# mLSTM head outputs: from "divide, square, normalise, gate" to "copy, square undivided, one factor with the gate"

## The chip, the cores and the metric

The kernel runs on one core of a Trainium2 chip. The metric is the device time of one execution in microseconds (us). TensorE (PE) multiplies matrices and writes its sums into PSUM, eight banks of 128 partitions by 512 fp32 numbers. VectorE (DVE), ScalarE (ACT) and GpSimd (POOL) work between PSUM and SBUF; SyncE's queue (SP) issues the transfers.

## The reference, cut to what matters

Two transformer blocks on 256 tokens of width 1024, all in fp32. The change lies in the first mixer of the second block, the mLSTM with four heads of 128 columns:

```
s   = einsum(q, k) * exp(d - m_t)
num = einsum(s, v) ;  den = sum(s)
h   = num / max(|den|, exp(-m_t))            # (256 tokens, 4 heads, 128)
hm  = rmsnorm(h, head_gain) * sigmoid(mo)    # mean of squares over the 128 columns of a head
out = concat([hm, stick_breaking_heads]) @ w_out
```

## The kernel before, in words

All tokens are handled at once, as two tiles (t = 0, 1) of 128 tokens on the 128 partitions. Every weight matrix comes through a ring of four 1 MB slots (SP, line 251) and is split into a high and a low part of reduced precision, in parts of 128x1024: ACT copies the high part (line 279), DVE subtracts to get the low part (line 282), and PE makes three products per tile of weights (line 303 for products that give columns, lines 365 and 383 for products that give rows). PE is in order and so are the others, and each engine's list is written out by hand.

The mixer's stage is a list of slots s = 0 to 18 (`ab_pe`, `ab_act`, `ab_dve`). In each slot ACT and DVE first split one weight part (the one that PE uses some parts later), and then do a step of the heads that is due there. PE runs one part of a weight product and then `after(s)`, the heads' small matmuls. Slots 0 to 7 go with eight parts of the product with the weights of the stick-breaking queries and keys, slots 8 to 11 with the row product `ab_sv`, slots 12 to 18 with the row product `ab_out`, which takes the heads' outputs as its left side. Heads n = 0 to 3 are mLSTM, 4 to 7 stick-breaking.

The names that matter:

- `first(n)`, `second(n)` (lines 1322 to 1342): a head's first two small products, into banks 4 and 5. `weigh(n)` (lines 1354 to 1356): the head's weights times its values, into bank 6: for an mLSTM head 2 x 129 columns, the 129th being `den`. Since there is one bank 6, `weigh(n)` waits until `ab_o` says that head n-1 has been taken out.
- `finish(n)` on DVE, in slots 3 to 6: takes bank 6 out. It makes `max(|den|, exp(-m_t))` in two small instructions (lines 1565, 1567), its reciprocal (1568), and one multiply for each tile out of the bank (1570); the last of them raises `ab_o`.
- `head_squares_dve` in slot 7: two squares of 128x512 (1610) and two sums (1611), each waited for, and then `ab_ssq`. ACT makes `exp(-0.5 ln(mean + eps))` of it (1480, 1481) and only then goes on to slot 8, whose first work is the split of the last part of `ab_sv`.
- `head_gate_dve` in slots 8 and 9, one tile in each: times the norm's factor (1618), times the gate `SGM` (1619), then `ab_om`.
- `turn(c)` on PE after slots 10 and 11 (1373): transposes heads c and c+1 of both tiles; it waits for `ab_om` = 2, for both c. `turn(0)` stands in PE's list ahead of the last 24 matmuls of `ab_sv` (line 383), and ahead of it stands `first(6)` (1326), which waits for the last weight part of `ab_sv` (line 282, slot 8). ACT (`high`, 1453) and DVE (`low`, 1576) take the turned heads out.

Of the kernel before, what the change touches and what calls it, by code (L numbers as in the profile page):

```python
# [5 lines left out]
P = 128  # L6
T = 256
TT = T // P
# [11 lines left out]
ALU = mybir.AluOpType  # L20
ACT = mybir.ActivationFunctionType
# [81 lines left out]
def build_two_blocks(nc, I, out):  # L103
# [9 lines left out]
    with ExitStack() as ctx:  # L113
# [93 lines left out]
        def named(name):  # L207
            if name not in S:
                S[name] = sem(name)
            return S[name]  # L210
# [3 lines left out]
        def act_then(ins):  # L214

            chain_n["act"] += 1
            ins.then_inc(s_act_chain, 1)
            nc.scalar.wait_ge(s_act_chain, chain_n["act"])
# [1052 lines left out]
        L3 = MIX[:, 768:1536].rearrange("p (a n) -> p a n", a=2)  # L1271
        SP3 = view(70 * 256, (2, 384))
        W3 = view(73 * 256, (2, 384))
        HSQ = view(65 * 256, (TT, 4, P))
        HST = view(69 * 256, (4, 8))
        GC = view(62 * 256, (TT, 36))
        DN = view(63 * 256, (4, 2, 2))
        SQK_TILE = (0, 4, 2, 6)
        NSL = 12
        FIRST_AT = {0: 0, 1: 1, 2: 2, 3: 3, 5: 4, 6: 5, 9: 6, 11: 7}  # L1280
# [14 lines left out]
        def ab_pe():  # L1295
# [67 lines left out]
                mm.then_inc(named("ab_pv"), 1)  # L1363

            def turn(c):
                pe.wait_ge(named("ab_om"), 2)
                if c:
                    pe.wait_ge(named("ab_tl"), 1)
                else:
                    pe.wait_ge(named("ab_row"), 5)  # L1370
                for i in range(2):
                    for t in range(TT):
                        mm = pe.transpose(PS[:, 7, i * T + t * P:i * T + (t + 1) * P],
                                          OM2[:, t, (c + i) * P:(c + i + 1) * P], ident[:, :])
                mm.then_inc(named("ab_tp"), 1)
# [40 lines left out]
        def ab_act():  # L1416
            cols_done(act, "ab_mqk", 0)
            act.activation(ABT[:, 8:10, :], PS[:, A, :].rearrange("p (c n) -> p c n", c=2),
                           ACT.Copy).then_inc(named("ab_ca"), 1)
            split_through(act, "ab_g", 3)  # L1420
            act.wait_ge(named("ab_row"), 1)
            act.activation(ROWSG[0:4, 1, :], ROWSG[0:4, 0, :], ACT.Tanh, scale=1.0 / 15).then_inc(named("ab_log"), 1)
            act.preload_act_table_set(EXP_LN)
            act.wait_ge(named("ab_row"), 2)
            act_then(act.activation(ROWSG[0:4, 4, :], ROWSG[0:4, 3, :], ACT.Exp))
            act.activation(ROWSG[0:4, 5, :], ROWSG[0:4, 4, :], ACT.Ln, bias=one_c[0:4, 0:1]).then_inc(named("ab_log"), 1)
            split_through(act, "ab_g", 4)
            act.wait_ge(named("ab_row"), 3)
            act.activation(GA[32:36, :], ROWSG[0:4, 9, :], ACT.Exp, scale=-1.0).then_inc(named("ab_log"), 1)
            for t in range(TT):  # L1430
                rows_done(act, "ab_vo", 2 * t + 1)
                act.activation(SGM[:, t, :], PS[:, G + 2 * t + 1, :], ACT.Sigmoid).then_inc(named("ab_sgm"), 1)
            act.preload_act_table_set(EXP_LN)

            def soft(n):
                act.wait_ge(named("ab_u"), n + 1)
                if n < 4:
                    act.activation(L3[:, n % 2, :], U3[:, n % 2, :], ACT.Exp).then_inc(named("ab_l"), 1)
                    return
                if n >= 6:  # L1440
                    act.wait_ge(named("ab_sp"), n - 5)
                act_then(act.activation(L3[:, n % 2, :], U3[:, n % 2, :], ACT.Abs))
                act_then(act.activation(L3[:, n % 2, :], L3[:, n % 2, :], ACT.Exp, scale=-1.0))
                act.activation(L3[:, n % 2, :], L3[:, n % 2, :], ACT.Ln, bias=one_c[:, 0:1]).then_inc(named("ab_l"), 1)

            def exp_w(n):
                act.wait_ge(named("ab_sec_read"), n + 1)
                act.wait_ge(named("ab_pv"), n - 1)
                act.activation(W3[:, n % 2, :], U3[:, n % 2, :], ACT.Exp).then_inc(named("ab_w"), 1)

            def high(c):
                act.wait_ge(named("ab_tp"), c // 2 + 1)
                act.activation(ab_group(0, c), PS[:, 7, :].rearrange("p (c n) -> p c n", c=2),
                               ACT.Copy).then_inc(named("ab_th"), 1)

            def out_high(n):
                act.wait_ge(named("ab_pv"), n + 1)
                act.activation(ab_t(0, n), PS[:, 6, 0:T], ACT.Copy).then_inc(named("ab_oh"), 1)

            base = first_part[first_unit["ab_sqk"]]  # L1460
            for s in range(NSL + DC - 1):
                split(act, base + s + 3)
                if s < 8 and s % 2:
                    u, tile = s // 2, SQK_TILE[s // 2]
                    act.wait_ge(s_used, base + s + 1)
                    act.activation(ABT[:, tile:tile + 2, :], PS[:, u, :].rearrange("p (c n) -> p c n", c=2), ACT.Copy,
                                   scale=(1.0 if tile >= 4 else P ** -0.5)).then_inc(named("ab_ca"), 1)
                if s == NSL - 1:
                    for t in range(TT):
                        rows_done(act, "ab_sv", t)  # L1470
                        act.activation(SV[:, t, :], PS[:, G + t, :], ACT.Copy).then_inc(named("ab_svr"), 1)
                if s in EXP_W_AT:
                    exp_w(EXP_W_AT[s])
                if s in AB_WEIGH_AT and AB_WEIGH_AT[s] >= 4:
                    out_high(AB_WEIGH_AT[s])
                if s in FIRST_AT:
                    soft(FIRST_AT[s])
                if s == AB_SSQ_AT:
                    act.wait_ge(named("ab_ssq"), 1)
                    act_then(act.activation(HST[:, 1, :], HST[:, 0, :], ACT.Ln, bias=eps_c[:, 0:1], scale=1.0 / P))  # L1480
                    act.activation(HST[:, 2, :], HST[:, 1, :], ACT.Exp, scale=-0.5).then_inc(named("ab_hrs"), 1)
                if s in AB_TURN_AT:
                    high(AB_TURN_AT[s])

        def ab_dve():
# [73 lines left out]

            def finish(n):  # L1560
                dve.wait_ge(named("ab_pv"), n + 1)
                o = PS[:, 6, 0:258].rearrange("p (t n) -> p t n", t=2)
                dn = DN[:, n, :, :]

                dve_then(dve.scalar_tensor_tensor(out=dn[:, 0, :], in0=o[:, :, 128], scalar=-1.0,
                                                  in1=GC[:, :, 32 + n], op0=ALU.mult, op1=ALU.max))
                dve_then(dve.tensor_tensor(dn[:, 0, :], o[:, :, 128], dn[:, 0, :], ALU.max))
                dve_then(dve.reciprocal(dn[:, 1, :], dn[:, 0, :]))
                for t in range(TT):
                    ins = dve.tensor_scalar(OM2[:, t, n * P:(n + 1) * P], o[:, t, 0:P], dn[:, 1, t:t + 1], None,  # L1570
                                            ALU.mult)
                ins.then_inc(named("ab_o"), 1)

            def low(c):
                dve.wait_ge(named("ab_th"), c // 2 + 1)
# [9 lines left out]
            for s in range(NSL + DC - 1):  # L1585
# [7 lines left out]
                if s in AB_FINISH_AT:  # L1593
                    finish(AB_FINISH_AT[s])
                if s == AB_SSQ_AT:
                    dve.wait_ge(named("ab_o"), 4)
                    head_squares_dve(OM2, HSQ, HST, 4, "ab_ssq")
                if s in AB_GATE_AT:
                    dve.wait_ge(named("ab_hrs"), 1)
                    dve.wait_ge(named("gate_gain"), 2)  # L1600
                    head_gate_dve(OM2, AB_GATE_AT[s], HST, 4, SGM, "ab_om")
                if s in AB_TURN_AT:
                    low(AB_TURN_AT[s])
                if s in AB_WEIGH_AT and AB_WEIGH_AT[s] >= 4:
                    out_low(AB_WEIGH_AT[s])

        def head_squares_dve(o_all, sq, st, heads, told):
            for t in range(TT):
                o = o_all[:, t, :].rearrange("p (h d) -> p h d", h=heads)
                dve_then(dve.tensor_tensor(sq[:, t, :, :], o, o, ALU.mult))  # L1610
                dve_then(dve.tensor_reduce(st[:, 0, heads * t:heads * (t + 1)], sq[:, t, :, :], AX.X, ALU.add))
            dve.sem_inc(named(told), 1)

        def head_gate_dve(o_all, t, st, heads, gate, done):

            o = o_all[:, t, :].rearrange("p (h d) -> p h d", h=heads)
            r = st[:, 2, heads * t:heads * (t + 1)].unsqueeze(2).to_broadcast([P, heads, P])
            dve_then(dve.tensor_tensor(o, o, r, ALU.mult))
            dve.tensor_tensor(o, o, gate[:, t, :].rearrange("p (h d) -> p h d", h=heads),
                              ALU.mult).then_inc(named(done), 1)  # L1620

        def gate_gain_pool(gate, gain, heads, sem_name, per_tile, told):

# [1179 lines left out]
```

## Time and profile before

| | |
|---|---|
| median of 3 runs | 1328.74 us (1327.57 to 1329.91) |
| profiled execution, its own time | 1329.45 us |
| its span, first to last instruction | 1327.6 us |
| mean granted clock of TensorE | 0.985 of full |
| the mixer's slots 0 to 18, in the span | about 447 to 532 us |

The profiled execution took 0.71 us more than the median of the runs, and 1.85 us of its time lie outside its span. Sums of instruction times are made against the profiled execution; the median is used to place them among the runs.

### The profile page before, as it was taken

What the parts mean: (1) busy time and instruction counts of PE and PEld (TensorE: products, weight loads), DVE (VectorE), ACT (ScalarE), POOL (GpSimd) and SP (SyncE); (2) the same over time, 40 slices, a digit from 0 to 9 for tenths busy, and PEclk for the clock granted to TensorE, in tenths of its full rate; (3) what the DMA queues carried; (4) which work ended last, traced back from release to release, by engine and by line L of the source; (5) the groups of instructions that cost most, each with busy time, mean ns of one, the idle gap of its engine ahead of it and who ended that gap; (6) DMA issues with size and microseconds to landing.
All of it is one profiled execution on the core that took longest, in us unless ns stands there. A gap on an engine that the chain in (4) does not pass through costs nothing.

```text
span 1327.6 us, 22040 instructions
## 1 busy us (share of the span) xinstructions
PE 1271.8 (96%) x9160; PEld 1152.9 (87%) x9160; DVE 792.4 (60%) x1163; ACT 707.6 (53%) x1118; POOL 128.3 (10%) x146
## 2 busy tenths in 40 slices
PE   6999999999999989999999999998999999999997
PEld 6988899998888877888999888987998888999886
DVE  5786678885456555645555446786645635655444
ACT  6767666664476534644655335554355634655433
POOL 6000001110000000000111000105600000111000
PEclk9999999999999998999999999998999999999999
DMA  9433465555544523543555555532203534465550
GB/s 335 161 117 107 143 191 187 176 180 196 188 138 175 190 69 137 175 143 112 169 182 189 191 177 159 183 120 92 92 8 111 190 128 139 149 189 190 191 191 32
DMA packets 141430, 205.52 MB, mean 155 GB/s; under 512 B 3730, under 2 KB 118802, under 8 KB 141330
## 3 DMA queue, kind: packets, MB, share of 16 engines
q1 hardware_dynamic: 141330, 204.11, 46.5%
q8 instruction: 72, 1.18, 0.4%
q14 instruction: 28, 0.23, 0.0%
HBM read 203.05 MB, written 1.05 MB: 154 GB/s over the span
## 4 chain that ended last, share of the span: by engine, by line
PE 84%; DVE 7%; ACT 5%; issue 2%; POOL 1%; DMA 1%; SPq 0%; DVEq 0%; ACTq 0%; POOLq 0%
PE ps L303 40%; PE ps L365 27%; PE ps L383 5%; PE ps L2080 2%; DVE weights_lo L282 2%; PE ps L1705 1%; ACT weights_hi L279 1%; PE ps L2142 1%; PE ps L1727 1%; PE ps L487 1%; POOL arena L2368 1%; DVE split_arena L518 1%; ACT normed L904 1%; DMA weights<-in_w_in 1%; PE ps L755 0%
## 5 line engine op out<-in xcount | busy, mean ns | idle before, releaser
L282 DVE TENSOR_TENSOR weights_lo<-weights,weights_hi 128x1024 fp32r<-128x1024 f32 x379 | 471.4, 1255 | 253.5 <-ACT weights_hi L279 251.3
L303 PE MATMUL ps<-split_arena,weights_hi 128*128 128x256 f32 x3056 | 561.8, 286 | 8.5 <-DVE split_arena L518 6.8
L279 ACT ACTIVATE weights_hi<-weights 128x1024 fp32r<-128x1024 f32 x379 | 396.7, 1056 | 274.3 <-PE ps L365 182.7
L303 PEld LDWEIGHTS ps<-split_arena,weights_hi 128*128 128x128 f32 x3056 | 479.3, 193 | 17.2 <-issue 12.0
L303 PE MATMUL ps<-split_arena,weights_lo 128*128 128x256 f32 x1528 | 433.4, 284 | 0.0
L303 PEld LDWEIGHTS ps<-split_arena,weights_lo 128*128 128x128 f32 x1528 | 294.4, 193 | 0.0
L365 PE MATMUL ps<-weights_hi,split_arena 128*128 128x512 f32 x992 | 272.7, 392 | 2.4 <-ACTq L1877 1.6
L365 PEld LDWEIGHTS ps<-weights_hi,split_arena 128*128 128x128 f32 x992 | 184.5, 188 | 41.7 <-issue 2.9
L365 PE MATMUL ps<-weights_lo,split_arena 128*128 128x512 f32 x496 | 153.7, 390 | 0.0
L365 PEld LDWEIGHTS ps<-weights_lo,split_arena 128*128 128x128 f32 x496 | 93.1, 188 | 19.7
L1885 POOL TENSOR_TENSOR normed<-normed 128x512 f32<-128x512 f32 x32 | 34.1, 1065 | 502.0 <-ACTq L1877 502.0
L1893 DVE TENSOR_TENSOR split_arena<-normed,split_arena 128x512 fp32r<-128x512 f32 x32 | 22.2, 693 | 73.8 <-POOL normed L1885 73.8
L383 PE MATMUL ps<-weights_hi,split_arena 128*128 128x512 f32 x192 | 62.6, 399 | 0.0
L1875 ACT ACTIVATE normed<-ps 128x512 f32<-128x512 f32 x32 | 19.1, 597 | 53.5 <-PE ps L303 53.5
L1188 POOL TENSOR_TENSOR arena<-arena 128x512 f32<-128x512 f32 x11 | 21.9, 1993 | 257.9 <-ACT arena L1133 163.1
L1171 DVE SCALAR_TENSOR_TENSOR arena<-ps,conv_cols,arena 128x255 f32<-128x255 f32 (+1 forms) x88 | 38.4, 478 | 13.7 <-ACT arena L1145 12.9
L383 PEld LDWEIGHTS ps<-weights_hi,split_arena 128*128 128x128 f32 x192 | 37.2, 194 | 7.9
L1145 ACT ACTIVATE arena<-ps,conv_cols 128x256 f32<-128x256 f32 x44 | 22.4, 560 | 37.8 <-PE ps L303 37.8
L303 PE MATMUL ps<-mem_t_hi,weights_hi 128*128 128x256 f32 x128 | 38.2, 299 | 3.3 <-DVE weights_lo L282 3.3
L518 DVE SCALAR_TENSOR_TENSOR split_arena<-ps,ln_cols,split_arena 128x256 fp32r<-128x256 f32 x72 | 29.5, 475 | 16.8 <-ACT split_arena L501 16.8
L2409 DVE SCALAR_TENSOR_TENSOR arena<-ps,cconv_cols,arena 128x255 f32<-128x255 f32 (+2 forms) x72 | 31.4, 477 | 13.4 <-ACT arena L2234 12.5
L383 PE MATMUL ps<-weights_lo,split_arena 128*128 128x512 f32 x96 | 38.3, 399 | 0.0
(364 smaller groups left out, 1321.3 us busy)
## 6 DMA issues: line engine op xcount, KB each, us to landing
weights<-in_mlp_w SPq DMA_DIRECT2D x64, 1024.0 KB, 5.3
weights<-in_w_up SPq DMA_DIRECT2D x22, 1024.0 KB, 5.1
weights<-in_c_w_in SPq DMA_DIRECT2D x16, 1024.0 KB, 5.4
weights<-in_w_in SPq DMA_DIRECT2D x14, 1024.0 KB, 6.3
weights<-in_ab_w_in SPq DMA_DIRECT2D x12, 1024.0 KB, 5.3
weights<-in_w_down SPq DMA_DIRECT2D x11, 1024.0 KB, 4.9
weights<-in_xa_wv SPq DMA_DIRECT2D x8, 1024.0 KB, 4.9
weights<-in_xa_wq SPq DMA_DIRECT2D x8, 1024.0 KB, 5.2
```

The source lines that it names most:

```text
L279: act.activation(h, r, ACT.Copy).then_inc(s_hi, 1)
L282: dve.tensor_tensor(l, r, h.bitcast(F32), ALU.subtract).then_inc(s_lo, 1)
L303: mm = pe.matmul(o, w[:, k, :], x[:, k, :], start=(k == 0 and i == 0), stop=(k == DC - 1 and i == 2))
L365: mm = pe.matmul(PS[:, banks[nb * t + b], :], x[:, t * P:(t + 1) * P], w[:, c:c + 512], start=(k == 0 and i == 0), stop=False)
L383: mm = pe.matmul(PS[:, banks[nb * t + b], :], x[:, t * P:(t + 1) * P], w[:, c:c + 512], start=(k == 0 and i == 0), stop=(k == chunks - 1 a ...
L518: ins = dve.scalar_tensor_tensor(out=dst[1][:, k, :], in0=PS[:, turn_bank(m) + c2, c * T:(c + 1) * T], scalar=ln_cols[:, gain, k:k + 1], i ...
L1145: ins = act.activation(CS[:, u % 4, f, :], PS[:, G + u % 4, f * T:(f + 1) * T], ACT.Identity, bias=c[:, 3:4], scale=c[:, 2:3])
L1171: ins = dve.scalar_tensor_tensor(out=CS[:, u % 4, f, lag:T], in0=PS[:, G + u % 4, f * T:(f + 1) * T - lag], scalar=c[:, tap:tap + 1], in1= ...
L1885: pool.tensor_tensor(RSQ[:, u % 2, :, :], RLU[:, u % 2, :, :], RLU[:, u % 2, :, :], ALU.mult).then_inc(named("m1_f"), 1)
L1893: dve.tensor_tensor(HID[1][:, 2 * u:2 * u + 2, :], RSQ[:, u % 2, :, :], HID[0][:, 2 * u:2 * u + 2, :].bitcast(F32), ALU.subtract).then_inc ...
L2080: mm = pe.matmul(PS[r, bank + hg, 64 * m:64 * m + 64], lhs(r, hg, m), rhs(r, hg, m), start=True, stop=True)
L2409: ins = dve.scalar_tensor_tensor(out=CC[:, u % 4, f, lag:T], in0=PS[:, G + u % 4, f * T:(f + 1) * T - lag], scalar=cconv_cols[:, TILE[u] + ...
```

## The change

`finish(n)` becomes one copy of the whole bank region, 258 columns, to the new tile `RAW`; the copy raises `ab_o`. Behind it DVE squares and sums the undivided numerators of the head, one `tensor_tensor_reduce` for each tile of tokens, which leaves the 128 squares in `OM2` (not used) and the sum in `HST`. `head_means` in slot 7 makes the four heads' denominators, reciprocals and mean squares together in five instructions on 128x8 numbers, since the norm of a divided head is that of the undivided one times the reciprocal squared. ACT's two small instructions stay. `head_gates(g)` in slots 8 and 9 multiplies norm factor and reciprocal into one factor for each head and tile, and applies it and the gate in one `scalar_tensor_tensor` per head and tile: heads 0 and 1 of both tiles in slot 8, heads 2 and 3 in slot 9 (before: all heads of tile 0, then of tile 1). `turn(0)` waits for the first of these groups only.

```diff
@@ -1271,10 +1271,10 @@
         L3 = MIX[:, 768:1536].rearrange("p (a n) -> p a n", a=2)
         SP3 = view(70 * 256, (2, 384))
         W3 = view(73 * 256, (2, 384))
-        HSQ = view(65 * 256, (TT, 4, P))
-        HST = view(69 * 256, (4, 8))
+        RAW = view(65 * 256, (4, TT, 129))
+        HST = view(69 * 256 + 16, (5, 4, TT))
         GC = view(62 * 256, (TT, 36))
-        DN = view(63 * 256, (4, 2, 2))
+        DN = view(63 * 256, (2, 4, TT))
         SQK_TILE = (0, 4, 2, 6)
         NSL = 12
         FIRST_AT = {0: 0, 1: 1, 2: 2, 3: 3, 5: 4, 6: 5, 9: 6, 11: 7}
@@ -1363,7 +1363,7 @@
                 mm.then_inc(named("ab_pv"), 1)
 
             def turn(c):
-                pe.wait_ge(named("ab_om"), 2)
+                pe.wait_ge(named("ab_om"), c // 2 + 1)
                 if c:
                     pe.wait_ge(named("ab_tl"), 1)
                 else:
@@ -1477,8 +1477,9 @@
                     soft(FIRST_AT[s])
                 if s == AB_SSQ_AT:
                     act.wait_ge(named("ab_ssq"), 1)
-                    act_then(act.activation(HST[:, 1, :], HST[:, 0, :], ACT.Ln, bias=eps_c[:, 0:1], scale=1.0 / P))
-                    act.activation(HST[:, 2, :], HST[:, 1, :], ACT.Exp, scale=-0.5).then_inc(named("ab_hrs"), 1)
+                    act_then(act.activation(HST[:, 3, :, :], HST[:, 2, :, :], ACT.Ln, bias=eps_c[:, 0:1],
+                                            scale=1.0 / P))
+                    act.activation(HST[:, 4, :, :], HST[:, 3, :, :], ACT.Exp, scale=-0.5).then_inc(named("ab_hrs"), 1)
                 if s in AB_TURN_AT:
                     high(AB_TURN_AT[s])
 
@@ -1559,17 +1560,39 @@
 
             def finish(n):
                 dve.wait_ge(named("ab_pv"), n + 1)
-                o = PS[:, 6, 0:258].rearrange("p (t n) -> p t n", t=2)
-                dn = DN[:, n, :, :]
-
-                dve_then(dve.scalar_tensor_tensor(out=dn[:, 0, :], in0=o[:, :, 128], scalar=-1.0,
-                                                  in1=GC[:, :, 32 + n], op0=ALU.mult, op1=ALU.max))
-                dve_then(dve.tensor_tensor(dn[:, 0, :], o[:, :, 128], dn[:, 0, :], ALU.max))
-                dve_then(dve.reciprocal(dn[:, 1, :], dn[:, 0, :]))
+                dve.tensor_copy(RAW[:, n, :, :],
+                                PS[:, 6, 0:258].rearrange("p (t n) -> p t n", t=TT)).then_inc(named("ab_o"), 1)
+                dve.wait_ge(named("ab_o"), n + 1)
                 for t in range(TT):
-                    ins = dve.tensor_scalar(OM2[:, t, n * P:(n + 1) * P], o[:, t, 0:P], dn[:, 1, t:t + 1], None,
-                                            ALU.mult)
-                ins.then_inc(named("ab_o"), 1)
+                    h = RAW[:, n, t, 0:P]
+                    ins = dve.tensor_tensor_reduce(out=OM2[:, t, n * P:(n + 1) * P], in0=h, in1=h, scale=1.0, scalar=0.0,
+                                                   op0=ALU.mult, op1=ALU.add, accum_out=HST[:, 0, n, t:t + 1])
+                if n == 3:
+                    dve_then(ins)
+
+            def head_means():
+                den = RAW[:, :, :, 128]
+                dve_then(dve.scalar_tensor_tensor(out=DN[:, 0, :, :], in0=den, scalar=-1.0,
+                                                  in1=GC[:, :, 32:36].rearrange("p t n -> p n t"),
+                                                  op0=ALU.mult, op1=ALU.max))
+                dve_then(dve.tensor_tensor(DN[:, 0, :, :], den, DN[:, 0, :, :], ALU.max))
+                dve_then(dve.reciprocal(DN[:, 1, :, :], DN[:, 0, :, :]))
+                dve_then(dve.tensor_tensor(HST[:, 1, :, :], HST[:, 0, :, :], DN[:, 1, :, :], ALU.mult))
+                dve.tensor_tensor(HST[:, 2, :, :], HST[:, 1, :, :], DN[:, 1, :, :],
+                                  ALU.mult).then_inc(named("ab_ssq"), 1)
+
+            def head_gates(g):
+                if g == 0:
+                    dve.wait_ge(named("ab_hrs"), 1)
+                    dve_then(dve.tensor_tensor(DN[:, 0, :, :], HST[:, 4, :, :], DN[:, 1, :, :], ALU.mult))
+                    dve.wait_ge(named("gate_gain"), 2)
+                for n in (2 * g, 2 * g + 1):
+                    for t in range(TT):
+                        cols = slice(n * P, (n + 1) * P)
+                        ins = dve.scalar_tensor_tensor(out=OM2[:, t, cols], in0=RAW[:, n, t, 0:P],
+                                                       scalar=DN[:, 0, n, t:t + 1], in1=SGM[:, t, cols],
+                                                       op0=ALU.mult, op1=ALU.mult)
+                ins.then_inc(named("ab_om"), 1)
 
             def low(c):
                 dve.wait_ge(named("ab_th"), c // 2 + 1)
@@ -1593,31 +1616,13 @@
                 if s in AB_FINISH_AT:
                     finish(AB_FINISH_AT[s])
                 if s == AB_SSQ_AT:
-                    dve.wait_ge(named("ab_o"), 4)
-                    head_squares_dve(OM2, HSQ, HST, 4, "ab_ssq")
+                    head_means()
                 if s in AB_GATE_AT:
-                    dve.wait_ge(named("ab_hrs"), 1)
-                    dve.wait_ge(named("gate_gain"), 2)
-                    head_gate_dve(OM2, AB_GATE_AT[s], HST, 4, SGM, "ab_om")
+                    head_gates(AB_GATE_AT[s])
                 if s in AB_TURN_AT:
                     low(AB_TURN_AT[s])
                 if s in AB_WEIGH_AT and AB_WEIGH_AT[s] >= 4:
                     out_low(AB_WEIGH_AT[s])
-
-        def head_squares_dve(o_all, sq, st, heads, told):
-            for t in range(TT):
-                o = o_all[:, t, :].rearrange("p (h d) -> p h d", h=heads)
-                dve_then(dve.tensor_tensor(sq[:, t, :, :], o, o, ALU.mult))
-                dve_then(dve.tensor_reduce(st[:, 0, heads * t:heads * (t + 1)], sq[:, t, :, :], AX.X, ALU.add))
-            dve.sem_inc(named(told), 1)
-
-        def head_gate_dve(o_all, t, st, heads, gate, done):
-
-            o = o_all[:, t, :].rearrange("p (h d) -> p h d", h=heads)
-            r = st[:, 2, heads * t:heads * (t + 1)].unsqueeze(2).to_broadcast([P, heads, P])
-            dve_then(dve.tensor_tensor(o, o, r, ALU.mult))
-            dve.tensor_tensor(o, o, gate[:, t, :].rearrange("p (h d) -> p h d", h=heads),
-                              ALU.mult).then_inc(named(done), 1)
 
         def gate_gain_pool(gate, gain, heads, sem_name, per_tile, told):
 
```

## Rows read from the trace of the kernel before

**Rows 1.** The page, part 4: the chain that ended last, by engine.

```profile
PE 84%; DVE 7%; ACT 5%; issue 2%; POOL 1%; DMA 1%; SPq 0%; DVEq 0%; ACTq 0%; POOLq 0%
```

**Rows 2.** Waits of PE, 440 to 532 us: us in total, times, longest.

```profile
PE ps L1373 <- DVE arena L1619: 4.1, 1, 4.1
PE ps L1354 <- DVE arena L1570: 3.0, 2, 1.8
PE ps L1326 <- DVE weights_lo L282: 1.0, 1, 1.0
PE ps L1336 <- DVEq L1544: 0.6, 1, 0.6
```

**Rows 3.** Windows of the stage: stretch, busy by engine, then PEclk, the granted clock.

```profile
450.00:458.50 8.50, 7.91 (x52) 6.85 (x51) 5.45 (x8) 4.22 (x7) 0.00 (x0) 1.00 0.37 123
...
468.00:472.50 4.50, 3.61 (x17) 3.64 (x18) 3.52 (x10) 1.14 (x2) 0.00 (x0) 0.62 0.25 36
...
501.00:509.50 8.50, 8.50 (x29) 6.93 (x30) 2.34 (x4) 2.82 (x5) 0.00 (x0) 0.67 0.34 123
```

**Rows 4.** Timeline of PE: start, us, line, what it is.

```profile
495.85 0.70 PE L1326 MATMUL ps<-arena 128*128 128x256 f32 x2 [1.04 <-DVE weights_lo L282]
```

**Rows 5.** The chain in order of time: start, us, what.

```profile
468.89 0.67 PE ps L1354 x2
...
470.42 3.79 PE ps L303 x24
...
480.26 0.46 PE ps L1354 x2
...
481.17 2.87 PE ps L303 x24
...
500.88 1.11 PE ps L1373 x4
501.99 7.63 PE ps L383 x24
...
511.15 0.44 PE ps L1373 x4
511.58 5.46 PE ps L365 x24
```

**Rows 6.** Timeline of DVE, same columns as group 4.

```profile
467.55 0.15 DVE L1565 SCALAR_TENSOR_TENSOR arena<-ps,arena 128x2 f32<-128x2 f32 x1
...
468.13 0.61 DVE L1570 TENSOR_SCALAR arena<-ps,arena 128x128 f32<-128x128 f32 x2
...
490.11 0.68 DVE L1610 TENSOR_TENSOR arena<-arena 128x512 f32<-128x512 f32 x1
...
495.72 0.55 DVE L1556 SCALAR_TENSOR_TENSOR normed<-ps,normed 128x384 f32<-128x384 f32 x1
...
500.13 0.69 DVE L1619 TENSOR_TENSOR arena<-arena 128x512 f32<-128x512 f32 x1
```

**Rows 7.** Timeline of ACT, same columns as group 4.

```profile
493.05 0.30 ACT L1480 ACTIVATE arena<-arena,eps_c 128x8 f32<-128x8 f32 x1 [2.30 <-DVEq L1612]
...
493.50 1.05 ACT L279 ACTIVATE weights_hi<-weights 128x1024 fp32r<-128x1024 f32 x1
...
499.53 0.52 ACT L1442 ACTIVATE normed<-normed 128x384 f32<-128x384 f32 x1 [1.76 <-DVE normed L1533]
...
502.11 0.58 ACT L1453 ACTIVATE split_arena<-ps 128x512 fp32r<-128x512 f32 x1
```

**Rows 8.** DVE by line and form over the span: count, busy, mean ns, idle before.

```profile
L1021 DVE CUSTOM_DVE_ANT_0 normed<-ps,arena 128x128 f32<-128x128 f32 x20 | 5.7, 285 | 0.0
...
L1021 DVE DVE_READ_ACCUMULATOR2_ANT arena<- 128x1 f32 x40 | 3.3, 83 | 0.0
...
L1651 DVE COPY arena<-ps 128x256 f32<-128x256 f32 x5 | 2.1, 419 | 4.5 <-PE ps L303 4.5
...
L1036 DVE SCALAR_TENSOR_TENSOR normed<-normed,arena 128x128 f32<-128x128 f32 x4 | 1.4, 348 | 0.1
```

## The prediction, made before the changed kernel was run

> **What bounds the kernel now.** I read the page's chain first: PE holds 84% of what ended last [rows 1], so what counts in a stage is where PE stands still, and at which clock it runs. Then PE's waits in the changed stage, 440 to 532 us. There are five stops, 8.8 us together [rows 2]: 4.1 us ahead of turn(0) (line 1373), for the second tile's gate; 3.0 us in two stops ahead of weigh(1) and weigh(3) (1354), for the divide of the head before; 1.0 us ahead of first(6) (1326), for a weight split; 0.6 us ahead of a second(n) (1336), which the change doesn't touch. Then the granted clock: 1.00 from 450 to 458.5 us, but 0.62 from 468 to 472.5 and 0.67 from 501 to 509.5 [rows 3], part of each stretch at the lower of the two levels (1.2 instead of 2.4 GHz). Both times PE had just stood: 1.19 us (what 3.0 leaves beside the 1.85 ahead of weigh(3); the times of the stops follow from the rows of DVE and the chain) and 4.10 us. The chain gives the price as the same work at both levels [rows 5]. Last I read DVE's and ACT's timelines, for what is late ahead of each stop [rows 6, 7].
>
> **The copy out of the bank.** Before, DVE's finish takes from 467.55 to 468.74 (468.13 plus 0.61) [rows 6], and weigh(1) starts at 468.89 [rows 5], 0.15 later. Now one copy stands there. The nearest row is a copy of 128x256 out of PSUM, 0.42 us [rows 8]; two more columns add nothing that matters. The bank is free at 467.55 + 0.42 = 467.97, and PE starts at 468.12: **0.77 us** gained. The third finish has the same form, so weigh(3) gains the same, **0.76 us**. The two stops shrink to about 0.4 and 1.1 us. If the copy cost as much as a 128x512 instruction (0.68 [rows 6]), 0.5 would be left of each gain; so 0.5 to 0.8 each.
>
> **The squares behind the copy.** Two instructions of the kind at line 1021, 0.285 us at 128x128, each with a read of the accumulator, 0.083 [rows 8]. End to end that is 0.74 us at most; overlapped as the neighbours in the timeline overlap (0.08 each), about 0.55. With the copy and a wait for it, some 1.05 to 1.25 us, against 1.19 before: DVE is as long in finish as it was, but bank 6 is no longer behind it. What would be late next is the DVE split of the next slot; it isn't later than before.
>
> **The means.** head_squares runs from 490.11 [rows 6], and ACT's Ln starts at 493.05 [rows 7]: 2.94 us with the handover, of which 0.08 is the handover. Now there are five small chained instructions on 128x8. Three of that kind took from 467.55 to 468.13 [rows 6], 0.193 each, so 0.97 together (0.8 if only the instructions counted, 1.25 if strided operands cost a quarter more). Ln starts at 490.11 + 0.97 + 0.08 = 491.16, which is 1.89 earlier. ACT's two small ones and the split that stands behind them [rows 7], and then DVE's split, all come 1.89 earlier. The split ended at 495.79 before (PE starts 0.06 later, 495.85 [rows 4]), so at 493.9 now. PE is through with its preceding matmuls at 495.85 - 1.04 = 494.81: it doesn't wait, and the whole stop ahead of first(6) goes, **1.04 us**.
>
> **The gates.** first(6) then runs from 494.81 to 495.74 (it took from 495.85 to 496.78, the 4.10 us ahead of 500.88 taken off). DVE: after_second(5), at 495.72 before [rows 6], is at 493.83 and ends at 494.30 (0.55 less the overlap); one small product, 0.2; four scalar_tensor_tensor of 128x128, 0.348 each by line 1036 [rows 8], 0.27 apart with the overlap: 1.16. The first group is done at 495.66, end to end without overlap at 496.0. PE was released at 500.88 by an instruction that ended at 500.82 [rows 5, 6]; now it is released at 495.72 to 496.1, against its own 495.74. So 4.10 us become 0 to 0.35; I take 0.2 and a gain of **3.9 us**. Three things make it: less work in slot 7, only half of the gating ahead of turn(0), and that slot 9's split and after_first(6), which stood between the two gate calls, are no longer ahead of it. DVE's work over the whole change is about 10 us before and 8.5 after; alone it would be worth nothing.
>
> A rule that speaks against eight short gates instead of four long ones: the Trainium skill, "VectorE: DVE Perf Modes", section "The TRN2 errata", says that each instruction on SBUF operands pays a fixed latency, so that large tiles are to be preferred. The trace agrees: 0.348 us for 128 columns against 0.69 for 512. By rule and row the gating takes 2.8 us as it did before; it is the order and not the amount that I count on.
>
> **The clock.** From 468.89 to 470.42 PE did weigh(1) at the lower level, 1.53 us; the same at the higher one is 480.26 to 481.17, 0.91. The 24 matmuls behind took 3.79 against 2.87 [rows 5]. Together 1.54 us. After turn(0)'s stop: 1.11 against 0.44 and 7.63 against 5.46, together 2.84 us [rows 5]. If nothing of the long stop is left, the second goes; I take **2.8 us**. For the first, the row to go by is the stop of 0.6 us ahead of line 1336 [rows 2], after the same kind of small matmuls on 4 and 64 rows: the clock stayed at 1.00 [rows 3]. The stop is 0.4 now, so I take that it stays up, **1.5 us**. The Trainium skill, "TensorE: Matmul & The Clock Gate", section "What's actually happening", has it that the lower level is the default and that activity releases it; by that the second is given back, and of the first it says less than the row.
>
> **What could be late next.** PE now comes to the end of line 383's matmuls 7 us sooner than DVE and ACT were used to. Between first group and low(0) they have: DVE's split of slot 9, after_first(6), the second gate group; ACT's soft(6), its split and high(0), which took from 499.53 to 502.69 [rows 7]; then DVE's split, after_l(6), low(0). Put one behind another from 495.7, with 1.2 us for a DVE split (the distance of 2.67 from Ln to after_second less ACT's 0.45 and 1.05) and 0.5 for the short ones: soft(6) starts at 497.7, high(0) ends at 500.9, low(0) ends at about 502.7. PE needs sp(6) at 495.9 + 0.4 + 5.5 + 0.6 = 502.4 and the low part at 503.3. That is just enough. In slot 12 the same chain is some 0.2 us late ahead of second(7). I count **0.3 us** lost, 0 to 3.
>
> **The sum.** 0.77 + 0.76 + 1.04 + 3.9 + 1.5 + 2.8 - 0.3 = 10.5 us. The profiled execution took 1329.45 us, so 1318.95, its span 1317.1. That execution was 0.71 above the median of 1328.74; from the median it is 1318.2. I forecast **1318.5 us**. The transfers don't bind here: each weight slot is asked for four units ahead, and no stop of PE in the stage ends with a DMA [rows 2].
>
> **The rivals.**
> - The clock falls once all the same, after what is left of weigh(1)'s stop or somewhere new, since a shift by 10 us moves all later work: 1.5 to 2.8 us less, **1320 to 1321.5**. For it: it fell after only 1.19 us. Against: the stop of 0.6.
> - DVE and ACT become the bound of slots 9 to 12, by the thin margin above; the stop moves to second(6), turn(2) or second(7). 3 us, and with them a stretch at the lower level, 1.5: **1321.5 to 1323.5**. A stop in the same place by a gate group that is a microsecond longer than by my rows gives the same.
> - It is slower: the new square instruction is much dearer between a copy and a wait than at line 1021. Place: behind the copy in slots 3 to 6, where eight of them stand ahead of the DVE splits that PE needs. The gains of 10.5 are used up, and more, when eight cost over 1.4 us each beyond their 0.29 (11.2 us in all, if nothing covers them): at 2 us each, **1332**. Nothing in the rows of line 1021 speaks for it.
> - No change: turn(0) is released no sooner, as something else than the gates holds it. Then only the copy and the first clock stretch count, 1 to 3 us, **1326 to 1328**. Against: PE's stop ends 0.06 us after the last gate.
>
> **How the numbers follow.** Forecast 0.60, 1316.5 to 1320. Clock once 0.20; late chain 0.13; no change 0.05, slower 0.02. The range, 1315.5 to 1323.0, takes in the first three but for their edges; below it is what a luckier clock in the rest of the kernel could give, one stretch of 1.5. A change of 0.2% (2.7 us) is about what measurements of this kernel can tell from none. Faster 0.95, same 0.03, slower 0.02.
>
> **What would show it.** PE's waits in the stage: the 4.1 ahead of turn(0) under 0.5, none ahead of first(6), about 0.4 and 1.1 ahead of weigh(1) and weigh(3). ACT's Ln about 1.9 us sooner after after_second(4). The granted clock 1.00 from weigh(1) to turn(2). If a new stop stands ahead of second(6), turn(2) or second(7), the second rival holds. The forecast is wrong if the first gate group ends over 0.5 us behind first(6), or if the clock falls without a stop.

## The result

The changed kernel takes 1319.70 us (median of 4 runs, 1317.09 to 1321.31), the kernel before 1329.33 us in the runs beside it (4 runs, 1327.57 to 1330.22): a ratio of 0.9927, 95% interval 0.9907 to 0.9948, so 9.6 us or 0.7% faster. The profiled execution of the changed kernel took 1320.48 us, with a span of 1318.8.

PE's waits in the same stage of the changed kernel (us in total, times, longest), to be read against [rows 2]:

```profile
PE ps L1354 <- DVE arena L1563: 1.5, 2, 1.1
PE ps L1336 <- DVEq L1545: 0.6, 1, 0.6
PE ps L1373 <- DVE arena L1592: 0.3, 1, 0.3
```

The stop ahead of turn(0) is 0.3 in place of 4.1 us, that ahead of first(6) is gone, the two ahead of weigh(1) and weigh(3) are half as long, and the one that the change didn't touch is as it was. Stops in the stage went from 8.8 to 2.4 us.

The windows of the changed kernel (busy by engine, then the granted clock), against [rows 3]:

```profile
450.00:521.40 71.40, 68.95 (x409) 59.80 (x408) 43.14 (x83) 34.64 (x53) 0.00 (x0) 1.00 0.39 128
468.00:472.50 4.50, 4.08 (x35) 3.96 (x34) 3.54 (x13) 1.52 (x3) 0.00 (x0) 1.00 0.16 15
```

The granted clock is 1.00 from end to end of the stage.

The whole times differ between runs of these two kernels by 3 and 4 us (by up to 7 for a variant below), so the stage is measured by itself, in the profile: from the start of the last 24 matmuls of `ab_vo`, the row product just ahead of slot 0 (line 383), to the start of the last 24 of `ab_out`. The stage of the two kernels was measured twice and repeats to 0.01 us, that of the variants below once. The chain of the kernel before (start, us, what) has the first here, the first matmuls of weigh(2), and the group that ends where the second begins, at 528.78 + 2.75 = 531.53:

```profile
441.68 5.45 PE ps L383 x24
...
474.21 0.23 PE ps L1354 x2
...
528.78 2.75 PE ps L365 x12
```

and the chain of the changed kernel:

```profile
442.14 5.45 PE ps L383 x24
...
468.57 0.46 PE ps L1354 x2
...
469.47 2.88 PE ps L303 x24
472.35 0.23 PE ps L1354 x2
...
477.63 0.46 PE ps L1354 x2
...
493.10 0.66 PE ps L1373 x4
493.76 5.48 PE ps L383 x24
...
500.76 0.44 PE ps L1373 x4
...
521.47 5.44 PE ps L383 x24
```

The stage takes 531.53 - 441.68 = 89.85 us before and 521.47 - 442.14 = 79.33 after: **10.52 us less**, against a forecast sum of 10.5.

### The profile page after: what moved, and what is told of

The parts are those of the page before. It is cut to its first block, busy times and chain, and to the rows that moved or that the text cites. A ratio compares the mean times of both kernels' runs of the same rounds, so it can differ in the third digit from the quotient of the medians.

```text
span 1318.8 us, 22045 instructions
## 1 busy us (share of the span) xinstructions
PE 1271.2 (96%) x9160; PEld 1152.8 (87%) x9160; DVE 789.5 (60%) x1169; ACT 707.4 (54%) x1118; POOL 127.7 (10%) x146
## 3 DMA queue, kind: packets, MB, share of 16 engines
HBM read 203.05 MB, written 1.05 MB: 155 GB/s over the span
## 4 chain that ended last, share of the span: by engine, by line
PE 84%; DVE 7%; ACT 5%; issue 2%; POOL 1%; DMA 1%; SPq 0%; DVEq 0%; ACTq 0%; POOLq 0%
PE ps L303 41%; PE ps L365 27%; PE ps L383 5%; DVE weights_lo L282 2%; PE ps L2085 2%; PE ps L1710 1%; ACT weights_hi L279 1%; PE ps L2147 1%; PE ps L1732 1%; PE ps L487 1%; POOL arena L2373 1%; DVE split_arena L518 1%; ACT normed L904 1%; DMA weights<-in_w_in 1%; PE ps L755 0%
## 5 line engine op out<-in xcount | busy, mean ns | idle before, releaser
L365 PE MATMUL ps<-weights_lo,split_arena 128*128 128x512 f32 x496 | 153.7, 390 | 0.0
L2373 POOL TENSOR_TENSOR arena<-arena,level_masks 64x512 f32<-64x512 f32 x24 | 34.1, 1420 | 42.2 <-DVEq L2483 34.6
```

Source lines behind the costliest of these rows:

```text
L365: mm = pe.matmul(PS[:, banks[nb * t + b], :], x[:, t * P:(t + 1) * P], w[:, c:c + 512], start=(k == 0 and i == 0), stop=False)
L2373: ins = pool.tensor_tensor(LT[r, lvl % 2, hg, :, :], ATC[r, hg, :, r], LM[r, lvl, r].unsqueeze(1).to_broadcast([64, 8, 64]), ALU.mult)
```

## Where the 10.5 us are, and the rest

The same chain gives the terms one by one, each as the distance between two starts, before and after:

| from, to | before | after | gained | forecast |
|---|---|---|---|---|
| start to weigh(1): its stop | 27.21 | 26.43 | 0.78 | 0.77 |
| weigh(1) to weigh(2): the clock | 5.32 | 3.78 | 1.54 | 1.5 |
| weigh(2) to weigh(3): its stop | 6.05 | 5.28 | 0.77 | 0.76 |
| weigh(3) to turn(0): two stops | 20.62 | 15.47 | 5.15 | 4.94 |
| turn(0) to turn(2): the clock | 10.27 | 7.66 | 2.61 | 2.8 |
| turn(2) to the end: late chain | 20.38 | 20.71 | -0.33 | -0.3 |

The last row is where the forecast had it, ahead of second(7) (line 1341) in slot 12. second(7) waits for a step of DVE (line 1551) that ends at 506.60; it starts 0.10 us late and takes 0.88 in place of 0.65:

```profile
506.75 0.88 PE ps L1341 x2
```

DVE and ACT, to see that the steps are those of the forecast (timelines of the changed kernel, start, us, line, what, idle before it):

```profile
468.00 0.42 DVE L1563 COPY arena<-ps 128x258 f32<-128x258 f32 x1
468.45 0.29 DVE L1568 CUSTOM_DVE_ANT_0 arena<-arena 128x128 f32<-128x128 f32 x1
468.67 0.08 DVE L1568 DVE_READ_ACCUMULATOR2_ANT arena<- 128x1 f32 x1
...
487.55 0.16 DVE L1575 SCALAR_TENSOR_TENSOR arena<-arena 128x8 f32<-128x8 f32 x1
...
488.38 0.17 DVE L1581 TENSOR_TENSOR arena<-arena 128x8 f32<-128x8 f32 x1
...
491.91 1.14 DVE L1592 SCALAR_TENSOR_TENSOR arena<-arena 128x128 f32<-128x128 f32 x4
...
499.39 0.68 DVE L1599 TENSOR_TENSOR split_arena<-ps,split_arena 128x512 fp32r<-128x512 f32 x1
```

```profile
488.58 0.30 ACT L1480 ACTIVATE arena<-arena,eps_c 128x8 f32<-128x8 f32 x1 [0.39 <-DVE arena L1581]
```

The copy takes 0.42, a square 0.29 and its read 0.08; the whole finish is over at 468.96, 0.96 us after its start (forecast 1.05 to 1.25). The five small instructions of the means end 1.00 us after their start (487.55 to 488.55; forecast 0.97), and ACT's Ln starts 1.03 after it, where it was 2.94 before [rows 6, 7]. A group of gates takes 1.14 (forecast 1.16). The low part of the first turned heads is done at 500.07, 7.0 us after the first gates, as forecast, and it is there before PE asks.

The span fell by 8.8 and not by 10.5 us. 0.46 of the difference lies ahead of the stage, which began at 442.14 and not at 441.68, in work that the change doesn't touch. So the changed kernel was 10.06 us ahead at the end of the stage, and of these it lost 2.0 in one place, where both kernels do the same work. The windows there, as above, in the changed kernel and in the one before (10 us later):

```profile
795.00:815.00 20.00, 17.53 (x105) 15.89 (x104) 14.32 (x25) 12.21 (x27) 0.00 (x0) 0.83 0.40 126
```

```profile
805.00:825.00 20.00, 16.90 (x123) 15.43 (x122) 14.94 (x27) 13.95 (x30) 0.00 (x0) 1.00 0.46 140
```

The granted clock fell in the changed kernel (0.51 from 802 to 809) and not in the one before. Ahead of this place the same weight split of DVE starts at 794.78 against 804.69, 9.91 earlier; behind it the same split starts only 7.91 earlier, in the changed kernel and before:

```profile
818.89 1.21 DVE L282 TENSOR_TENSOR weights_lo<-weights,weights_hi 128x1024 fp32r<-128x1024 f32 x1
```

```profile
826.80 1.21 DVE L282 TENSOR_TENSOR weights_lo<-weights,weights_hi 128x1024 fp32r<-128x1024 f32 x1
```

The last 0.9 us of the 8.8 come behind the last instruction of DVE, which starts at 1314.43 against 1322.32, 7.89 earlier.

A second profile of the changed kernel has the same stage to the hundredth and a span of 1316.0 us. The clock falls in that place there too, for less long (0.91 over the 20 us from 793), and costs 1.2 us. Neither profile of the kernel before has this fall; of the eight variants below five have it and three have not. So its length differs between executions, and whether the shift by 10 us brings it about is open.

## The experiments

Each kernel's stage is measured as above. Rival 1 throughout is that the gain is DVE work taken away. Not in the table: 0.6 us ahead of second(1) in all but the last two, and 0.8 ahead of second(5) with finish first.

| kernel | stage, us | stops at weigh(n) | at first(6)+turn(0) | whole kernel against before |
|---|---|---|---|---|
| before, twice | 89.85, 89.84 | 3.0 | 5.1 | |
| changed, twice | 79.33, 79.33 | 1.5 | 0.3 | 0.9927 (0.9907 to 0.9948) |
| copy alone | 85.84 | 1.5 | 5.2 | 0.9970 (0.9960 to 0.9979) |
| pairs alone | 82.71 | 3.0 | 2.0 | 0.9953 (0.9939 to 0.9968) |
| changed, both pairs awaited | 83.62 | 1.5 | 3.3 | 0.9953 (0.9934 to 0.9972) |
| changed, bank freed late | 81.94 | 2.6 | 0.3 | 0.9941 (0.9924 to 0.9958) |
| changed, means 1.4 later | 80.82 | 1.5 | 1.5 | 0.9930 (0.9913 to 0.9947) |
| changed, means 2.8 later | 82.95 | 1.5 | 2.6 | 0.9947 (0.9927 to 0.9967) |
| changed, finish first | 79.04 | 0.2 | 0.8 | 0.9919 (0.9905 to 0.9933) |
| changed, copy first | 78.20 | 0.3 | 0.8 | 0.9907 (0.9892 to 0.9922) |

### The copy alone

```diff
-                o = PS[:, 6, 0:258].rearrange("p (t n) -> p t n", t=2)
+                dve.tensor_copy(RAW[:, n, :, :],
+                                PS[:, 6, 0:258].rearrange("p (t n) -> p t n", t=TT)).then_inc(named("ab_o"), 1)
+                dve.wait_ge(named("ab_o"), n + 1)
+                o = RAW[:, n, :, :]
...
-                ins.then_inc(named("ab_o"), 1)
```

> The kernel before, with the copy out of the bank alone: finish(n) copies 258 columns to RAW and raises ab_o, and then does the old divide out of RAW; squares, sums and gates as before. The measure is the stage: from the start of the last 24 matmuls of ab_vo (line 383) to the start of the last 24 of ab_out, 89.85 us before and 79.33 with the change. My theory (PE's stops and the clock behind them): both stops ahead of weigh(n) shrink from 3.0 to 1.5 us, the granted clock stays at 1.00 behind weigh(1), and the stage takes 86.8 us (3.0 less); the 4.1 and the 1.0 ahead of turn(0) and first(6) stay as they are, and so does the lower clock behind turn(0). Rival 1 (it is the DVE work taken away that counts): DVE has 2.5 us more to do here, so the stage is not shorter, or longer. Rival 2 (the clock behind weigh(1) was chance): 88.3 us.

Its waits (lines lie one further down) and chain:

```profile
PE ps L1374 <- DVE arena L1623: 4.1, 1, 4.1
PE ps L1355 <- DVE arena L1563: 1.5, 2, 1.1
```

```profile
443.04 5.45 PE ps L383 x24
...
500.34 6.64 PE ps L383 x24
...
528.88 5.44 PE ps L383 x24
```

The stage takes 528.88 - 443.04 = 85.84 us, 4.0 less, though DVE has more to do than before: a finish takes 1.53 us in place of 1.19, so 1.4 more for the four (not the 2.5 that I expected). Both stops are those of the changed kernel and the clock stays up behind weigh(1): 3.0 us as expected. The further 1.0 is not the copy's: the stop ahead of turn(0) is 4.1 as before, but the 24 matmuls behind it took 6.64 and not 7.63 us, for the clock came back sooner, behind the same stop. That was luck of this execution as far as is known. Rival 1 falls here with the 3.0 alone.

### The pairs alone

```diff
-                pe.wait_ge(named("ab_om"), 2)
+                pe.wait_ge(named("ab_om"), c // 2 + 1)
...
+            cols = slice(256 * g, 256 * (g + 1))
+            for t in range(TT):
+                o = o_all[:, t, cols].rearrange("p (h d) -> p h d", h=2)
...
+                ins = dve.tensor_tensor(o, o, gate[:, t, cols], ALU.mult)
+            ins.then_inc(named(done), 1)
```

> The kernel before, with the gates in the other order alone: in slot 8 heads 0 and 1 of both tiles, in slot 9 heads 2 and 3, with the same two multiplies on the same number of columns (four instructions of 128x256 in place of two of 128x512), and turn(0) waits for the first pair only. My theory: turn(0) is released at the end of slot 8's gates, so the stop of 4.1 us shrinks to about 1.1; the stop of 1.0 ahead of first(6) stays; the clock behind stays up, or falls for less long. The stage takes 84.0 us with the clock kept, 86.8 with the old fall. Rival 1 (less DVE work is what counts): DVE's work is not less, so 89.85 or a little more.

```profile
PE ps L1354 <- DVE arena L1570: 3.0, 2, 1.8
...
PE ps L1373 <- DVE arena L1625: 1.0, 1, 1.0
```

```profile
441.82 5.45 PE ps L383 x24
...
469.94 2.87 PE ps L303 x24
...
497.07 5.48 PE ps L383 x24
...
524.53 5.44 PE ps L383 x24
```

The stage takes 82.71 us, 7.1 less, with the same multiplies on the same columns. The stop ahead of turn(0) is 1.0, and the 24 matmuls behind it take 5.48 us: the clock is kept. This is 1.3 less than the 84.0 that I expected, and the place is weigh(1): the stops ahead of weigh(n) are as before, 1.19 of the 3.0 us ahead of weigh(1), and yet the 24 matmuls behind it took 2.87 and not 3.79 us. So a stop of 1.19 us does not always bring the clock down, and 1.5 of the 7.1 us are not due to the order of the gates. From weigh(3) to turn(0) it takes 17.52 us, where it took 20.62 before and 15.47 with the change: the order gives 3.10, and the cheaper means and gates on top of it the other 2.05.

### The changed kernel with both pairs awaited

```diff
-                pe.wait_ge(named("ab_om"), c // 2 + 1)
+                pe.wait_ge(named("ab_om"), 2)
```

> The changed kernel, with turn(0) waiting for both pairs of heads (ab_om = 2) as before; all else as changed. My theory: turn(0) is released by the last gate of slot 9, which ended 3.0 us after that of slot 8, so its stop grows from 0.3 to 3.3 us and the stage from 79.33 to 82.3 us; if a stop of that length lets the clock fall, another 2.8, 85.1. Rival 1 (less DVE work is what counts): the DVE work is that of the change, so 79.3 to 80.

The stop ahead of turn(0) is 3.3 us; the chain:

```profile
442.74 5.45 PE ps L383 x24
...
497.40 7.05 PE ps L383 x24
...
526.36 5.44 PE ps L383 x24
```

The stage is 83.62 us, 4.3 more than with the change and with the same DVE work: rival 1 falls once more. 3.0 us are the stop, 7.05 - 5.48 = 1.6 the clock behind it, and the 0.33 us of the late chain come back. The lower clock was on for a shorter time than I had as the second case.

### The changed kernel with the bank freed behind the squares

```diff
-                dve.tensor_copy(RAW[:, n, :, :],
-                                PS[:, 6, 0:258].rearrange("p (t n) -> p t n", t=TT)).then_inc(named("ab_o"), 1)
-                dve.wait_ge(named("ab_o"), n + 1)
+                dve_then(dve.tensor_copy(RAW[:, n, :, :],
+                                         PS[:, 6, 0:258].rearrange("p (t n) -> p t n", t=TT)))
...
+                ins.then_inc(named("ab_o"), 1)
```

> The changed kernel, with ab_o raised by the last of the two squares and not by the copy; all else as changed. My theory: bank 6 comes free 0.5 to 0.6 us later, the two stops ahead of weigh(1) and weigh(3) grow from 1.5 to 2.6 us together, and the stage to 80.4 us; with the stop ahead of weigh(1) at 1.0 us the clock may fall behind it as it did before the change, then 81.9. Rival 1 (less DVE work is what counts): same work, same 79.3.

```profile
PE ps L1354 <- DVE arena L1567: 2.6, 2, 1.6
```

```profile
442.09 5.45 PE ps L383 x24
...
470.23 4.14 PE ps L303 x24
...
524.03 5.44 PE ps L383 x24
```

The stage takes 81.94 us: 1.1 of stops and 1.5 of clock, as in the second case. The stop ahead of weigh(1) was 1.0 here (2.6 less the 1.6 ahead of weigh(3)), and the 24 matmuls behind it took 4.14 us. The clock didn't fall in the stop but after it: weigh(1)'s three groups took 0.46, 0.26 and 0.43 us, where they took 0.46, 0.22 and 0.22 with the change.

### The means later, by 1.4 and by 2.8 us

```diff
                 den = RAW[:, :, :, 128]
+                for _ in range(2):
+                    dve_then(dve.tensor_tensor(OM2[:, 0, :], OM2[:, 0, :], OM2[:, 0, :], ALU.max))
```

and `range(4)`.

> The changed kernel, with two chained maxima of a tile with itself, 128x512, ahead of the five small instructions of head_means (on OM2, which holds nothing that is used at that point): 1.4 us more DVE work in slot 7, about as much work as the old squares and sums took beyond the new ones. My theory: first(6) had 0.6 to 0.7 us in hand, so it stops 0.7 us; turn(0) is released 1.4 us later; both stops together grow from 0.3 to 1.7 us, the stage from 79.33 to 80.7 us, and the clock stays up. A rival (DVE's idle time ahead of its weight splits covers it): the stage stays at 79.3.

> The same with four maxima, 2.8 us. My theory: the stops ahead of first(6) and turn(0) are 3.1 us together, the stage 82.1 us with the clock kept; if it falls behind them, up to 2.8 more, 84.9. Which of the two it is tells how much of the 2.8 us that I counted for the clock goes with the length of the stop, since the change took away 4.9 us of stops there at once.

The waits with 1.4 us more:

```profile
PE ps L1373 <- DVE arena L1594: 0.8, 1, 0.8
PE ps L1326 <- DVE weights_lo L282: 0.7, 1, 0.7
```

with 2.8 us more, and the 24 matmuls behind turn(0) in that kernel's chain:

```profile
PE ps L1326 <- DVE weights_lo L282: 2.1, 1, 2.1
...
PE ps L1373 <- DVE arena L1594: 0.5, 1, 0.5
```

```profile
497.51 6.05 PE ps L383 x24
```

With 1.4 us the stage is 522.19 - 441.37 = 80.82, 1.5 longer, first in first(6) and then in turn(0), and the clock stays up. With 2.8 it is 525.47 - 442.52 = 82.95, 3.6 longer: 2.9 up to the start of turn(0), and 1.0 behind it, where the clock had fallen (6.05 against 5.48 and the transposes ahead, 1.12 against 0.66), less the 0.33 us of the late chain. So what slot 7 costs on DVE comes at full length up to turn(0), and the 1.9 us that the cheaper means won there are won on PE's path. Of the clock's 2.6 us behind turn(0) none is lost with stops of 0.7 and 0.8 us, and 1.0 with 2.1 and 0.5.

### Finish ahead of after_first

The order of DVE's list changes in two places, so this run can't tell what each is worth.

```diff
+                if s == 1:
+                    after_l(AFTER_L_AT[s])
                 split(dve, base + s + 3)
...
+                if s in AB_FINISH_AT:
+                    finish(AB_FINISH_AT[s])
                 if s in FIRST_AT:
                     after_first(FIRST_AT[s])
```

> A version that should beat both: the changed kernel with DVE's list in other order in the mixer's slots. finish(n) stands ahead of after_first, so that the copy in slots 3 and 5 no longer waits for PE's first(3) and first(4), and in slot 1 the weighting (after_l(0)) stands ahead of the weight split. My theory: the stops ahead of weigh(1), 0.4, and weigh(3), 1.1, go, and the 0.6 ahead of line 1336; the stage takes 77.3 us (2.1 less than changed), the kernel about 1317.5 against 1319.7 us. A rival: DVE, which now squares ahead of after_first, gives ACT its input later, and the chain through ACT's split to turn(0) takes back what was gained, 78.5 to 79.3 us.

```profile
PE ps L1341 <- DVE normed L1557: 0.8, 1, 0.8
PE ps L1373 <- DVE arena L1592: 0.8, 1, 0.8
```

The stage takes 521.65 - 442.61 = 79.04 us: my theory was wrong and the rival right. The stops ahead of weigh(1), weigh(3) and second(1) are gone (0.2 us stand ahead of weigh(2)), but 0.8 us stand ahead of second(5) (line 1341) and 0.8 ahead of turn(0). From after_first(4) on the chain goes through DVE and ACT alone, up to turn(0).

### The copy alone ahead of after_first

```diff
+            def squares(n):
                 for t in range(TT):
                     h = RAW[:, n, t, 0:P]
...
+                if s == 1:
+                    after_l(AFTER_L_AT[s])
                 split(dve, base + s + 3)
...
+                if s in (3, 5):
+                    finish(AB_FINISH_AT[s])
...
                 if s in AB_FINISH_AT:
-                    finish(AB_FINISH_AT[s])
+                    if s not in (3, 5):
+                        finish(AB_FINISH_AT[s])
+                    squares(AB_FINISH_AT[s])
```

> The changed kernel; in slots 3 and 5 the copy alone stands ahead of after_first, the squares stay behind after_first and after_second, slots 4 and 6 are in the order of the change, and in slot 1 after_l(0) stands ahead of the weight split. Of the version with the whole of finish ahead, the chain showed why it won so little: from first(4) on DVE and ACT set the pace up to turn(0), with soft(4), ACT's split, DVE's split, after_l(4) and the third head's copy and squares ahead of after_first(5). My theory: the stops ahead of line 1336 (0.6) and weigh(1) (0.4) go whole; of the 1.1 ahead of weigh(3) only 0.5 is won, since after_first(5) can't be sooner than 5.7 us after first(4) (6.2 with the change); the stage takes 77.8 us, 1.5 less than with the change, the kernel about 1318 us. A rival (only PE's stops count): 77.2. Another (the chain takes all): 79.0.

PE's stops are 0.8 us ahead of turn(0) and 0.3 ahead of weigh(2). The chain around them:

```profile
471.42 0.44 DVE arena L1563
...
471.99 0.46 PE ps L1354 x2
...
476.53 0.57 DVE normed L1534
...
481.53 0.48 DVE normed L1534
```

The stage takes 520.79 - 442.59 = 78.20 us, 1.13 less than with the change, where I expected 1.5. From after_first(4) to after_first(5) (line 1534) it is 481.53 - 476.53 = 5.0 us (5.5 with the change), the 0.5 less that I expected; what fell short is ahead of it: PE, now earlier, stops 0.3 us ahead of weigh(2), whose bank is freed by the copy in slot 4, which I had left in its place. The whole kernel takes 1316.22 us (5 runs) against 1328.07 beside it. Its interval overlaps that of the change, so that it beats the changed kernel is shown by the stage only.

### Both kernels again

> The kernel before, unchanged, profiled once more, for the clock in the stage. If the lower clock behind weigh(1) and behind turn(0) belongs to the stops of 1.2 and 4.1 us, the stage takes 89.9 us again, with 3.8 us for the 24 matmuls behind weigh(1) and 7.6 for those behind turn(0). If it is partly a matter of how the stops fall, as the runs with the copy alone (6.6 us behind turn(0)) and with the pairs alone (no fall behind weigh(1) at a stop of 1.2) suggest, the stops are the same and the stage is 87.5 to 89.9.

> The changed kernel, unchanged, profiled once more. My theory: with no stop over 1.1 us in the stage the granted clock stays at 1.00 and the stage takes 79.3 us within 0.1, whatever the time of the whole. If the clock falls somewhere in it, the 1.5 us behind weigh(1) is not safely won.

The stages are 531.25 - 441.41 = 89.84 and 520.63 - 441.30 = 79.33 us. In the kernel before the clock fell in both places again, by 1.6 and 2.6 us against the changed one, and in that nowhere.

## Why the prediction was right

**What bounds.** That PE's stops and its clock decide the stage held in every run, up to the 0.3 us told below. The amount of DVE work decides nothing: more of it with the bank freed early made the stage 3.0 us shorter, beside 1.0 of clock, and the same work with a later wait made it 4.3 longer. It counts where it stands ahead of a release, as in slot 7. All of it fell further than forecast, from 10.4 us to 7.3 and not to 8.5 (finish, means and gates from the timelines).

**The copy** was forecast at 0.77 and 0.76 and gave 0.78 and 0.77; undoing its early release alone took 1.1 back.

**Means and gates** were forecast at 4.94 and gave 5.15. The stops themselves went from 5.14 to 0.27, 4.87; the other 0.3 is that matmuls right behind others overlap with them, which I had not counted: first(6) starts 0.16 us before the end of the matmuls ahead of it and takes 0.81 us, against 0.93 behind a stop. The gating takes 2.5 us (1.33 with the product of the factors, and 1.13) and not the 2.8 forecast, since gates of 0.35 us overlap. The slot order is the larger part: with it alone, the stop ahead of turn(0) was 1.0 in place of 4.1. The means were not run alone in the kernel before; what they are worth is shown from the other side, by the 1.4 and 2.8 us put back.

**The clock** behind turn(0) was forecast at 2.8 and gave 2.6, a term a little over its size; I had compared four transposes behind a stop, 1.11, with four behind other work, 0.44, where behind a short stop they take 0.66. Behind weigh(1) it gave the 1.54 forecast. But that it came was in part luck, for the ground that I gave was thin. The stop of 0.6 us that I went by comes behind four small matmuls on 4 rows (lines 1322 and 1323), and those on 64 rows stand behind it, not ahead; ahead of weigh(1) stand both kinds. And with the same stop of 1.19 us the clock fell in two profiles of the kernel before and not with the pairs alone. What can be said is that it fell in none of the profiles with a stop of 0.43 or less there. So 1.5 us of the 10.5 are what the change saves when the clock does fall, which the kernel before needn't do in each execution.

**The late chain** was forecast at 0.3 and cost 0.33, at the place forecast.

**The rivals.** The first had the clock fall once all the same, behind weigh(1) or somewhere new because of the shift, at 1.5 to 2.8 us. In the stage it did not come. In the profiled execution it came all the same, 280 us behind the stage, and cost 2.0 us: its time, 1320.48, lies in that rival's 1320 to 1321.5. My sum had no term for the clock outside the stage, neither down nor up, so its 10.5 us are right for the stage and 1.7 too many for this span. The median of 1319.70 stands between the forecast and the rival. The four runs go with the clock: 1317.09 us at a mean granted clock of 0.992, 1321.31 at 0.985. The second rival (DVE and ACT take 3 us back) did not come; the margin is as thin as said, and the two versions with another order ran into such a chain, but sooner in the stage than I had placed it, between first(4) and turn(0).

**The total.** 1318.5 was forecast, 1319.70 measured, inside 1315.5 to 1323.0. The 1.2 us between them are less than the 4.2 by which the four runs of the changed kernel differ, so that the total is met this closely is no proof of the terms; those rest on the stage.

## What to carry to other kernels

Price a change on a helper engine by the moment at which it releases the engine that bounds, and not by its work: free a PSUM bank with one copy and compute behind it, and order the elementwise work as its consumer takes it. A stop of the matmul engine costs more than its length when the clock falls behind it, so look at the same work at both levels; whether it falls could not be told from the length of the stop, so count it as a term that may not come. Measure the stage beside the whole, for the clock outside it moved the total by 1 to 2 us. After such a gain look for the chain that was hidden behind the stop: here it took back 1.8 of the 2.1 us that the first reordering after the change should have won.

## What the runs showed of the hardware

- Behind a stop of PE of 4.1 us the lower clock cost 2.6 us, 2.6 and 1.6 in three profiles (8.74, 8.73 and 7.76 us against 6.14 for the four transposes and the 24 matmuls), behind 3.3 us 1.6.
- Stops of 1.19 and 1.0 us ahead of weigh(1) were followed by a lower clock in three of four profiles, though PE had been fully busy for 10.2 us up to the stop (457.5 to 467.7 in the kernel before). Stops of 1.0 and 1.0, and of 0.7 and 0.8, around first(6) were followed by none, and neither was the longer one of 1.8 us (1.6 with the bank freed late) ahead of weigh(3) in the same four profiles. So the length of the stop does not decide it. What stood ahead of weigh(1) were eight small matmuls on 4 and 64 rows; that these matter was not tried.
- A `tensor_tensor_reduce` runs as two instructions, 0.29 us for 128 columns and 0.08 for the read of the sum, and the next one starts 0.22 us after it. Four of them, an estimate of 0.9 us, do for one tile what a square of 512 columns and its sum did in 1.4 (0.69 and 0.69).
- Two multiplies of 128x128 by one factor per partition took 0.61 us out of PSUM (line 1570 before) and 0.48 out of SBUF (with the copy alone).
